# Moving the decode prelude of a hybrid attention layer into the last steps of the prompt's attention

## The reference, cut to what matters

```
xn = rmsnorm(x, n1) * (1 + sc1) + sh1;  xn @ w_in -> q, three K/V pairs, gates, mLSTM q k v o, i/f
prompt : block (compressed), selected-block and window attention, mixed by sigmoid gates; mLSTM in chunks
decode : s  = q . block means of K            (16 blocks of 64 tokens; softmax p)
         o_cmp = p @ block means of V
         imp = p summed over the 4 query heads of a kv head  -> which blocks are selected
         o_sel = softmax(q . K of the selected blocks) @ V   (K, V in pages of the cache)
         o_win = softmax(q . K of the 512 window rows and the new rows) @ V
         a_out = g0 * o_cmp + g1 * o_sel + g2 * o_win
         mLSTM step from the states C, n, m; new states C, n, m are outputs
x = x + g1 * (concat(a_out, m_out) @ w_out);   then the ConvFFN (w_up, conv of width 3, silu, w_down)
```

## Time and profile before

| | us |
|---|---|
| runs: median (lowest to highest) | 1843.24 (1840.3 to 1852.04) |
| profiled execution, its own time | 1839.4 |
| its span | 1837.6 |
| PE busy in it | 1702.5 (93%) |
| PEld busy | 1530.9 (83%) |
| DVE busy | 919.6 (50%) |
| ACT busy | 610.8 (33%) |
| POOL busy | 186.7 (10%) |
| first matmul of layer 0's output projection | 454.77 |
| the same of layer 1 | 1336.75 |

### The profile page before, as it was taken

One profiled execution on the slowest core, in us unless ns is written; L12 is line 12 of the kernel. 1 busy time (PEld: TensorE's weight loads), 2 busy tenths in 40 slices (PEclk: granted clock), 3 DMA queues, 4 the chain that ended last, 5 costly groups with the idle time before them and its releaser, 6 DMA issues.

```text
span 1837.6 us, 37174 instructions
## 1 busy us (share of the span) xinstructions
PE 1702.5 (93%) x14719; PEld 1530.9 (83%) x14719; DVE 919.6 (50%) x2374; ACT 610.8 (33%) x1165; POOL 186.7 (10%) x304
## 2 busy tenths in 40 slices
PE   5899999977989999999989999898798999999996
PEld 3899875545989999999989997655588999999995
DVE  2544435646465645546463353474545555655644
ACT  2422225534142323224152212463323322422313
POOL 1001003433000000000000100154210000000001
PEclk9899978988989999999989997898998999999998
DMA  8435267478412222221122535633751222221201
GB/s 296 120 97 181 85 249 249 132 223 200 88 68 72 92 92 91 91 90 47 49 82 90 178 107 181 218 110 132 222 113 47 92 93 90 93 83 54 91 23 54
DMA packets 157876, 218.98 MB, mean 119 GB/s; under 512 B 11722, under 2 KB 116490, under 8 KB 157548
## 3 DMA queue, kind: packets, MB, share of 16 engines
q1 hardware_dynamic: 150096, 199.22, 34.3%
q0 software_dynamic: 7648, 17.94, 3.6%
HBM read 200.45 MB, written 16.68 MB: 118 GB/s over the span
## 4 chain that ended last, share of the span: by engine, by line
PE 85%; DVE 5%; ACT 3%; SPq 2%; issue 2%; DMA 2%; POOL 1%; DVEq 0%; ACTq 0%
PE ps L1237 28%; PE ps L1263 15%; PE ps L809 13%; PE ps L1197 6%; PE ps L683 3%; PE ps L854 2%; PE ps L920 2%; PE ps L935 2%; PE ps L890 1%; PE ps L795 1%; PE ps L1217 1%; PE ps L804 1%; PE ps L803 1%; SPq L546 1%; DMA work<-in_x_sample 1%
## 5 line engine op out<-in xcount | busy, mean ns | idle before, releaser
L1237 PE MATMUL ps<-work_r,big_r 128*128 128x272 f32 x1344 | 279.4, 289 | 5.5 <-issue 5.2
L1237 PE MATMUL ps<-work_r,slab_r 128*128 128x272 f32 x1344 | 278.7, 288 | 0.0
L1237 PE MATMUL ps<-xnT_r,big_r 128*128 128x272 f32 x1344 | 276.7, 287 | 0.0
L1237 PEld LDWEIGHTS ps<-work_r,big_r 128*128 128x128 f32 x1344 | 210.3, 188 | 8.1 <-issue 8.1
L809 PE MATMUL ps<-slab_r,work_r 128*128 128x256 f32 (+1 forms) x976 | 213.1, 285 | 0.0
L1237 PEld LDWEIGHTS ps<-xnT_r,big_r 128*128 128x128 f32 x1344 | 211.8, 188 | 0.0
L1237 PEld LDWEIGHTS ps<-work_r,slab_r 128*128 128x128 f32 x1344 | 210.7, 188 | 0.0
L1727 DVE TENSOR_TENSOR slab_r<-slab,big_r 128x2048 fp32r<-128x2048 f32 (+1 forms) x84 | 170.2, 2036 | 48.3 <-ACT big_r L1606 44.2
L809 PEld LDWEIGHTS ps<-slab_r,work_r 128*128 128x128 f32 x976 | 163.1, 191 | 2.7 <-issue 2.5
L1625 ACT ACTIVATE big<-big,work 128x560 f32<-128x560 f32 x44 | 33.6, 764 | 371.8 <-DVE big L2321 371.8
L1263 PE MATMUL ps<-side_r,big_r 128*128 128x272 f32 x704 | 148.1, 292 | 4.9 <-DVE big_r L1727 4.9
(11 more groups left out here) (446 smaller groups left out, 3215.8 us busy)
## 6 DMA issues: line engine op xcount, KB each, us to landing
slab<-in_w_mod SPq DMA_DIRECT2D x23, 2048.0 KB, 9.0
slab<-in_w_up SPq DMA_DIRECT2D x44, 1024.0 KB, 7.5
slab<-in_w_in SPq DMA_DIRECT2D x20, 1024.0 KB, 5.5
slab<-in_w_down SPq DMA_DIRECT2D x20, 1024.0 KB, 5.9
slab<-in_cache_cmp_kv SPq DMA_DIRECT2D x128, 128.0 KB, 2.0
slab<-in_cache_sel_kv SPq DMA_DIRECT2D x96, 128.0 KB, 2.0
big<-in_cache_win_kv SPq DMA_DIRECT2D x16, 512.0 KB, 5.5
out<-big POOLq DMA_DIRECT2D x16, 448.0 KB
```

The source lines that it names most:

```text
L1237: ins = mm(ps[2 * half + b][:, 0:HALF], wt, fr(x[:, k, HALF * b:HALF * b + HALF]), start=k == 0 and n == 0, stop=k == KC - 1 and n == 2)
```

## The change

- `FENCES` is `(12,)`: the barrier behind the attention is gone on all four engines. POOL waits in its place for its own stores up to there (`all_stored()`).
- PE's prelude moves into the attention: `decode_heads_turned` (L980 to L985) into step 22, `decode_block_scores` (L1005, L1011) into step 26, all in bank `ps[7]`. DVE's part goes to steps 21 (clearing of `Qbd` and `P4`), 23 (queries), 24 (gates), 27 (highest block score) and 29 (probabilities and `P4`), ACT's two exponents to step 28. The new DVE functions `decode_queries`, `decode_gates`, `decode_block_shift` and `decode_block_probs` hold the instructions of L2065 to L2078, L2087 to L2088 and L2127 to L2137, the queries with one wait and read from `ps[7]`.
- Right behind the attention PE sums the probabilities and turns `P4`, then turns the output gates (into banks 2, 3, 4, 1), then stacks the mLSTM heads (bank 6, once ACT has copied the last group out of it). Nothing waits for `d_cp` between the rounds of keys any more.
- SP issues the 16 pages of sequences 6 and 7 first, then the 8 loads of window rows.
- DVE finds the masked block ahead of its first key copy and waits for the norm gain (`gst_in`) later; ACT copies the turned `P4` and the first keys ahead of the exponent of the mLSTM decay.
- `P4`, `qTs`, `Qbd`, `KN`, `imp` and `small` move to a part of `work` that the attention doesn't use; `PTs` lands where prompt outputs are stored from, so ACT and DVE wait for these stores ahead of their first `probs_out`.

```diff
@@ buffers and fences
-        PTs = w(9, 128)
+        w.at = 7680
         P4 = w(2, 128)
         qTs, Qbd, KN = w(4, TS), w(NB, 32), w(2, TS)
-        cmb, imp, small = w(2, 128), w(2, 16), w(128)
+        imp, small = w(2, 16), w(128)
+        PTs = w(9, 128)
+        cmb = w(2, 128)
-        FENCES = (8, 12)
+        FENCES = (12,)
@@ SP
                 sp.wait_ge(mx_t.sem, mx_t.at(4, L))
+                for c in (6, 7):
+                    pages(spg[c], sel_pool, c, spg_in[c // 2])
                 for b in range(NB):
                     sp.dma_start(wpg[b]..., A["cache_win_kv"][L][b]...).then_inc(wpg_in[b // 4], 16)
-                    if b == 3:
-                        for c in (6, 7):
-                            pages(spg[c], sel_pool, c, spg_in[c // 2])
@@ PE, attention steps and what follows
                 for s in range(32):
                     turn(s)
...
                     if s % 4 == 0 and s:
                         values(s // 4 - 1)
+                    if s == 22:
+                        decode_heads_turned()
+                    if s == 26:
+                        decode_block_scores()
...
                 values(7)
-                pe.drain().then_inc(stage_done, 1)
-                pe.wait_ge(stage_done, stage_end(8, L))
+                pe.wait_ge(d_cp.sem, d_cp.at(1, L))
+                mm(ps[7][:, 416:448], K["samegroup"], imp[...], start=True, stop=True)
+                for j in range(2):
+                    ins = tr(ps[5][:, 128 * j:128 * j + 128], P4[:, j, :], ident)
+                ins.then_inc(d_imp.sem, 1)
                 for n in range(4):
...
-                        ins = tr(ps[n][:, 128 * t:128 * t + 128], proj[:, t, c:c + 128], ident)
+                        ins = tr(ps[(2, 3, 4, 1)[n]][:, 128 * t:128 * t + 128], proj[:, t, c:c + 128], ident)
                     ins.then_inc(mx_t.sem, 1)
-                for g in range(AG):
-                    tr(ps[4][:, TS * g:TS * g + TS],
-                       proj_s[:, 128 * g:128 * g + 128], idn(TS))
...
-                pe.wait_ge(mx_c.sem, mx_c.at(4, L))
+                pe.wait_ge(a_oc.sem, a_oc.at(AG, L))
...
                 ins.then_inc(ms_m.sem, 1)
-                pe.wait_ge(d_q.sem, d_q.at(1, L))
...
+                pe.wait_ge(mx_c.sem, mx_c.at(4, L))
@@ PE, rounds of keys
                 turn_keys(0, 0)
                 turn_keys(0, 1)
-                pe.wait_ge(d_cp.sem, d_cp.at(1, L))
...
                 turn_keys(0, 2)
@@ ACT
+                    if s == 28:
+                        act.wait_ge(d_csub.sem, d_csub.at(1, L))
+                        for j in range(2):
+                            ins = A_(imp[:, j, :], ps[7][:, 256 + 16 * j:272 + 16 * j], ACT.Exp, bias=small[:, j:j + 1],
+                                     accum_out=small[:, 2 + j:3 + j])
+                        ins.then_inc(d_cexp.sem, 1)
                 group_out(3)
-                act.drain().then_inc(stage_done, 1)
-                act.wait_ge(stage_done, stage_end(8, L))
@@ DVE
+                def decode_block_probs():
+                    dve.wait_ge(d_cexp.sem, d_cexp.at(1, L))
+                    V.reciprocal(small[:, 4:6], small[:, 2:4])
+                    drain()
+                    tt(imp[:, :, :], imp[:, :, :], bc(small[:, 4:6], 2, 16), ALU.mult)
+                    drain()
+                    for j in range(2):
+                        for b in range(4):
...
+                            ins = ts_(to, imp[r, j, :]..., gq[r, j, 0:1], None, ALU.mult)
+                    ins.then_inc(d_cp.sem, 1)
...
-                dve.drain().then_inc(stage_done, 1)
-                dve.wait_ge(stage_done, stage_end(8, L))
+                    if s == 21:
+                        V.memset(Qbd[:, :, :], 0.0)
+                        V.memset(P4[:, :, :], 0.0)
+                    if s == 23:
+                        decode_queries()
+                    if s == 24:
+                        decode_gates()
+                    if s == 27:
+                        decode_block_shift()
+                    if s == 29:
+                        decode_block_probs()
@@ POOL
-                pool.drain().then_inc(stage_done, 1)
-                pool.wait_ge(stage_done, stage_end(8, L))
+                all_stored()
```

More of the change, by code:

```diff
@@ L1128, in _ @@
                 turn_keys(0, 1)
-                pe.wait_ge(d_cp.sem, d_cp.at(1, L))
-                mm(ps[7][:, 32:64], K["samegroup"], imp[:, :, :].rearrange("p j n -> p (j n)"), start=True, stop=True)
-                for j in range(2):
-                    ins = tr(ps[5][:, 128 * j:128 * j + 128], P4[:, j, :], ident)
-                ins.then_inc(d_imp.sem, 1)
                 turn_keys(0, 2)
@@ L1548, in probs_out @@
                         act.wait_ge(d_pv.sem, d_pv.at(u, L))
+                    else:
+                        act.wait_ge(stored, L * ST_ALL + PROMPT_STORED)
                     A_(PTs[:, 0:4, :].rearrange("p a b -> p (a b)"), ps[0][:, :], ACT.Copy)
                     A_(PTs[0:TS, 8, :], ps[7][0:TS, 128:256], ACT.Copy).then_inc(d_pta.sem, 1)
+                act.wait_ge(d_imp.sem, d_imp.at(1, L))
+                A_(PTd[:, :, :].rearrange("p j n -> p (j n)"), ps[5][:, 0:256], ACT.Copy).then_inc(d_ctc.sem, 1)
+                keys_out(0, 0)
                 act.wait_ge(ms_E.sem, ms_E.at(1, L))
                 A_(Es, Es, ACT.Exp, bias=Rst[:, 0:1]).then_inc(ms_W.sem, 1)
[L1554 to L1561 removed]
                 keys_out(0, 2)
@@ L2068, in _ @@
-                drain()
-                for k in range(KV):
-                    h_ = slice(64 * k, 64 * k + 64)
-                    cp(Qbd[h_, :, 16 * k:16 * k + 16].rearrange("p b (g t) -> p b g t", g=AG),
-                       qTs[h_, :, :].rearrange("p g (b t) -> p b g t", b=NB))
-                for g in range(2):
-                    pr = ps[5][:, 24 * g:24 * g + 24].rearrange("p (h b) -> p b h", b=3)
-                    tt(small[:, 64 + 24 * g:88 + 24 * g].rearrange("p (b h) -> p b h", b=3), pr, bc(K["hsel"], 1, 3), ALU.mult)
@@ L2076, in _ @@
-                dve.drain().then_inc(d_q.sem, 1)
-                for g in range(2):
-                    red(gq[:, g, :], small[:, 64 + 24 * g:88 + 24 * g].rearrange("p (b h) -> p b h", b=3), X, ALU.add)
-                dve.wait_ge(ms_m.sem, ms_m.at(1, L))
-                cp(Rst[:, :], ps[3][:, 0:4])
-                tt(Es, ps[3][:, 32:64], K["samebatch"], ALU.add)
-                cp(Vst, ps[3][:, 64:64 + VA])
-                cp(STs, ps[3][:, 384:384 + TS])
-                cp(MOst, ps[3][:, 256:384])
@@ new lines, in _ @@
+                V.memset(small[:, 32:64], 0.0)
+                drain()
+                for j in range(2):
+                    ts_(sel[:, j, :], tot[:, j, 1:16], small[:, 6 + j:7 + j], None, ALU.is_equal)
+                drain()
+                tt(sel, sel, bc(K["iota"], 1, 2), ALU.mult)
+                drain()
+                red(small[:, 16:18], sel, X, ALU.max)
+                drain()
+                for j in range(2):
+                    ts_(small[:, 33 + 16 * j:48 + 16 * j], K["iota"], small[:, 16 + j:17 + j], NEG, ALU.is_equal, ALU.mult)
@@ L2094, in keys_out @@
+                cp(Vst, ps[6][:, 64:64 + VA])
+                cp(STs, ps[6][:, 384:384 + TS])
+                cp(MOst, ps[6][:, 256:384])
+                dve.drain().then_inc(ms_E.sem, 1)
                 def keys_out(r, b):
@@ L2123, in probs_out @@
                         dve.wait_ge(d_pv.sem, d_pv.at(u, L))
+                    else:
+                        dve.wait_ge(stored, L * ST_ALL + PROMPT_STORED)
                     cp(PTs[:, 4:8, :].rearrange("p a b -> p (a b)"), ps[1][:, :]).then_inc(d_ptd.sem, 1)
-                dve.wait_ge(gst_in, L * 64 + 64)
-                dve.wait_ge(d_cexp.sem, d_cexp.at(1, L))
-                V.reciprocal(small[:, 4:6], small[:, 2:4])
-                drain()
-                tt(imp[:, :, :], imp[:, :, :], bc(small[:, 4:6], 2, 16), ALU.mult)
-                drain()
-                for j in range(2):
-                    for b in range(4):
-                        r = slice(32 * b, 32 * b + 32)
-                        to = P4[r, j, :].rearrange("p (l b h n) -> p b h l n", l=4, h=2, n=2)[:, 4 * j + b, :, :, :]
-                        ins = ts_(to, imp[r, j, :].rearrange("p (h l n) -> p h l n", h=2, l=4), gq[r, j, 0:1], None, ALU.mult)
-                ins.then_inc(d_cp.sem, 1)
                 keys_out(0, 1)
```

122 lines of the change are left out of this document (64 added, 58 removed).

## The result

The changed kernel took 1856.07 us (median of 6 runs, 1850.61 to 1859.25), the kernel before 1838.89 us beside it (6 runs, 1834.41 to 1852.04). The ratio is 1.0083 with a 95% interval of 1.0057 to 1.0108. So the sign of the sum was right and the time lies in the range of 1834 to 1859, but near its upper end and outside the 1843 to 1852 of the forecast's own case: the forecast was 7 us of loss, and the profiled executions differ by 14.7 us (1854.06 against 1839.4).

What follows compares the result with a forecast made beforehand. SP's order of issue and what the 16 DMA engines must move were taken to set the decode stage's end. Layer losses of 3.8 and 3.3 us gave +7.1, 1846.5 from the profiled 1839.4; from a middle of 1841, 1848 us, range 1834 to 1859.

Steps and rivals of the forecast that it cites:

- the forecast's own case: Whole kernel: window loads slowed by stores, states late, 1843 to 1852 us, most likely 1848; chance 0.45.
- Attention end, +3.4: Attention steps: turned heads 0.7, block scores 0.2 and step 29's products 2.5 us add 3.4 us (1.0 to 5).
- Barrier and freed waits: Behind the attention: barrier gives back 0.72 us; removed waits, 6 us together, give nothing, PE idling some 2.7 us for pages.
- Pages first: SP's queue: pages start at 388.9, 1.08 us each, and land at 407.1 to 407.3, 1.7 us earlier than before.
- Window loads: Ahead of round 5: second half, slowed by the first half's stores, lands at 423; round 5 starts 2.2 us later.
- States: Ahead of the numerator: states land at 437.6, wanted at 436.3; numerator 3.8 us later; layer 0 loses 3.3 us, layer 1 3.8.
- Clock: PE behind long idle times: a stretch at half clock, priced at 3 us per layer, only in the slowest rival (0.15).
- Stores first and a cold PE: Rival: window loads land at 425.6 behind stores, states 5.7 us late, PE at half clock; 1857 us, chance 0.15.
- Loads not slowed: Rival: second half of window rows lands by 419.4 despite stores, each layer gains 1.4 us; 1833 to 1840 us, chance 0.30.

Runs made afterwards that it cites:

- run 3: Changed kernel with SP's old load order (4 window loads, 16 pages, 4 window loads) and the probabilities moved from step 29 to step 31: 1848.25 us, ratio 1.0029.
- run 13: run 3 with 20 matmuls whose result nobody reads, issued on PE where it waits for the pages: 1846.43 us, ratio 1.0034.
- run 5: Changed kernel with POOL holding the second half of the window stores until the mLSTM states land, decode keys weighted ahead of this wait: 1849.16 us, ratio 1.0053.
- run 4: Kernel before with only the new load order (16 pages of sequences 6 and 7, then 8 window loads): 1847.91 us, ratio 1.0033.
- run 11: Kernel before with only SP's order changed: a window load behind every fourth of the 16 pages, the last four behind the pages: 1835.32 us, ratio 0.997.
- run 2: Changed kernel with the probabilities moved from step 29 to step 31: 1847.03 us, ratio 1.0033.
- run 8: run 2 with 9 matmuls nobody reads in PE's wait for the pages and 9 more ahead of the numerator: 1844.99 us, ratio 1.002.
- run 12: Changed kernel, probabilities in step 31, a window load behind each fourth page, 12 matmuls nobody reads in PE's wait for the pages: 1840.74 us, ratio 1.0005.

## Why the prediction was right in sign and short in size

**Attention end, +3.4: held.** Heads and block scores were put at 0.9 and cost 0.85; step 29 at 2.5, and it delays the last values by 2.2. Sum 3.05. Missing was what a PE that has waited does next: 1.7 us more for the values.

**Barrier and freed waits: held.** They gave nothing but 0.72 us. PE was ready at 403.74 and waited 5.72 us for the pages, not some 2.7. With run 3 this is stronger than forecast: pages to numerator grew by 3.9 us per layer under the old order, of which run 13 shows 1.4 to be the clock behind the merged wait; the 1.9 of the second sum of values come and go between kernels, and no run shows why.

**Pages first.** A page took 1.07 us of SP's time (forecast 1.08), but the queue started at 390.55 and not at 388.9: 0.87 us of this is the later start of the attention and most of the rest comes from the cold values. They arrived at 409.42, not at 407.3, so that nothing was gained against 409.04.

**Window loads: wrong in the safe direction.** The second half was put at 423 by turns between loads and stores. It was in by 421.68, when POOL issued its stores, although its issue began 2.1 us later than forecast: the stores of the first half, put at 415.2, moved nothing before 419.5, so the loads ran all but alone. The idle 0.92 us ahead of round 5 is ACT's, as before (0.93), and not ended by a DMA, as the prediction had said. Taking off the 0.87, round 5 is 0.4 us later than before and not 2.2. The Trainium skill (DMA: Bandwidth & Descriptors, Queues, rings and completion order) has the engines take turns between queues a packet at a time. The profile's packets do not show such turns where both queues had been issued to: 357 to none over 416 to 419.5, and none to 477 over 424.3 to 429. Whether the engines already had work from the silent queue is not shown.

**States: right mechanism; right total, later start.** Forecast 437.6, in fact 439.81, or 438.9 without the later start. From the issue of the window loads to the landing of the states the prediction had 32.0 us (405.6 to 437.6), and it took 32.1 (407.70 to 439.81): the sum of what the engines have to move was right, and luck in part, since the order within it was not. PE wanted the states 1.7 us earlier than forecast (435.48 less 0.87, against 436.3). The wait of 1.6 us became 4.43. Run 5 shows that the stores make it.

**Clock: the term left out.** The forecast put all rows at full clock and gave half clock to a rival with 0.15, at 3 us per layer. Read from the rows, per layer: 1.7 us in the last values, which delay SP and with it the whole chain of transfers, and 1.7 us in the numerator, 3.4 in all. That is 6.8 us, beside the 7.6 us by which the profiled execution is over the forecast of 1846.5. It is an attribution and not a measurement: the other terms, of about 1 us each and of both signs, happen to cancel nearly, and no run changed only this clock. One of them is that what lies behind the numerator took 1.4 us more in layer 0 beside the numerator's own 1.7. So the rival "Stores first and a cold PE" (1857) gave the better time, though its first half, stores ahead of the window loads, did not happen: the stores went ahead of the states.

**"Loads not slowed", 0.30: half true and worth nothing.** The window loads were hardly slowed, and the time thus freed was spent in waiting for states. The rival let the state loads win against stores as well; issued behind them, they did not.

## What to carry to other kernels

When a stage waits in several places for one late transfer, taking the early waits away does not shorten it; it makes one long wait out of them, and the engine may come out of it at half clock just where it is on the path. Price each wait that a change makes longer twice, once as time and once as a slow stretch behind it (1.7 us here in each of two places), and give the second a chance, since not every such wait was followed by half clock. And look at what a load will meet in the queues when it is moved: here the order of 24 issues of SP in each layer, with nothing else changed, was worth +7 us one way (run 4) and -6 the other (run 11), while the removed waits, 6 us in each layer, gave nothing that could be measured.

## What the runs showed of the hardware

- Two queues did not share the DMA engines evenly while both had been issued to. Stores issued at 415.74 moved their first packets at about 419.5, when the window loads ahead of them (1.32 MB over 416 to 419.5) were nearly done. State loads in packets of 512 B, issued from 424.23, moved none before 429 beside 477 packets of stores, then 995 beside 286 over 429 to 434. Their landing took a median of 9.5 us where it had taken 4.6.
- The same issues took SP more time where the loads stood behind stores: four state loads 8.28 us (3.58 before, 3.01 in run 5, 9.23 in run 4), six loads of `w_out` 6.35 us (3.70 before, 9.18 in run 5).
- A wait of 2.36 us on PE, at full clock up to there, was followed by half clock (0.50 over 383 to 386) in both layers. A wait of 2.93 us was followed by full clock in both layers of five kernels (before, after, runs 2, 8 and 12), and in the others in one layer or in none.
